# Filter taps and spectra taken out of PSUM one round earlier in the odd attentions, the last heads rotated in two parts, one weight tile loaded before the filter table

## The reference

```python
def odd_mixer(h, positions, w_in, w_out, ...):
    u = h @ w_in                                   # 256 x 3072
    # 4 differential heads: q, k normed and rotated, two softmaxes each
    o_c = diff_causal_attention(qc, kc, vc, lam)   # p0 - lam * p1, times v
    o_c = rms_norm(o_c, diff_subln) * (1.0 - lam_init)
    # 8 block-attention heads; with 256 tokens there is one block: plain causal softmax
    qm = apply_rope(rms_norm(m[:, :, 0], moba_qn), positions)
    km = apply_rope(rms_norm(m[:, :, 1], moba_kn), positions)
    o_d = moba_attention(qm, km, m[:, :, 2])
    return concat([o_c, o_d]) @ w_out

def hyena_filters(L, w1, b1, w2, b2, w3, freq):    # second block, weights only
    h = sin(freq[1] * (sin(freq[0] * (feats @ w1 + b1)) @ w2 + b2))
    h = (h @ w3).reshape(L, 2, 2, 512)             # the "taps"
    h = h * exp(-t * deltas)                       # the window
    k = concat([h[:, :, 0], 0, h[:0:-1, :, 1]])
    return k / (sum(abs(k)) + EPS)
# long_conv later multiplies by rfft(k): the "spectra"

mod = silu(c) @ ada_w[layer] + ada_b[layer]        # modulation rows of each layer
```

## Time and profile before

| | us |
|---|---|
| median of 3 runs | 2554.66 |
| lowest and highest | 2551.91, 2556.96 |
| the profiled execution's own time | 2556.27 |
| its span in the profile | 2555.0 |
| TensorE busy | 2423.8 (95%) |
| VectorE busy | 1792.0 (70%) |
| ScalarE busy | 1227.1 (48%) |
| GpSimd busy | 392.2 (15%) |

### The profile page before, as it was taken

One profiled execution on the slowest core, in us unless ns is written; L12 is line 12 of the kernel. 1 busy time (PEld: TensorE's weight loads), 2 busy tenths in 40 slices (PEclk: granted clock), 3 DMA queues, 4 the chain that ended last, 5 costly groups with the idle time before them and its releaser, 6 DMA issues.

```text
span 2555.0 us, 27667 instructions
## 1 busy us (share of the span) xinstructions
PE 2423.8 (95%) x11093; PEld 1796.7 (70%) x11093; DVE 1792.0 (70%) x2019; ACT 1227.1 (48%) x1453; POOL 392.2 (15%) x434
## 2 busy tenths in 40 slices
PE   6987999998899999999999989999999999999998
PEld 2455797644469877454798658787878787878786
DVE  4576577585459766355665348888888888888887
ACT  1142453222135431122443247676767676767675
POOL 1045371131027210044221000000000000000000
PEclk9978999996899999999999999999999999999999
DMA  7631468642056777203466339989898989898995
GB/s 302 268 148 50 165 264 306 232 162 97 33 206 231 302 284 294 91 1 132 174 256 230 128 115 343 368 322 368 317 368 321 369 321 368 322 366 321 368 347 216
DMA packets 50672, 631.01 MB, mean 247 GB/s; under 512 B 8696, under 2 KB 9385, under 8 KB 12713
## 3 DMA queue, kind: packets, MB, share of 16 engines
q1 hardware_dynamic: 44192, 619.47, 64.3%
q10 hardware_dynamic: 3960, 6.97, 0.8%
q0 software_dynamic: 2384, 2.73, 0.3%
HBM read 625.47 MB, written 3.67 MB: 246 GB/s over the span
## 4 chain that ended last, share of the span: by engine, by line
PE 81%; DVE 9%; ACT 3%; issue 3%; DMA 3%; POOL 1%; ACTq 0%; SPq 0%; DVEq 0%; POOLq 0%
PE psum L1137 18%; PE psum L1138 18%; PE psum L1139 18%; PE psum L1032 4%; PE psum L1005 4%; PE psum L2460 3%; DVE sbuf L702 3%; PE psum L2454 2%; PE psum L1221 2%; PE psum L2039 1%; PE psum L1172 1%; DMA ring<-in_t_ada 1%; PE psum L2951 1%; PE psum L742 1%; DVE ring_r L1132 1%
## 5 line engine op out<-in xcount | busy, mean ns | idle before, releaser
L1138 PE MATMUL psum<-ring_r,sc_r 128*128 128x512 f32 x1688 | 665.8, 394 | 0.0
L1132 DVE TENSOR_TENSOR ring_r<-ring,sbuf_r 128x2048 fp32r<-128x2048 f32 (+1 forms) x287 | 538.4, 1880 | 174.4 <-ACT sbuf_r L1123 173.3
L1123 ACT CAST sbuf_r<-ring 128x2048 fp32r<-128x2048 f32 (+1 forms) x287 | 445.5, 1555 | 347.7 <-PE psum L1139 259.8
L1132 DVE TENSOR_TENSOR ring_r<-ring,sc_r 128x2048 fp32r<-128x2048 f32 (+1 forms) x243 | 478.3, 1974 | 137.9 <-ACT sc_r L1123 137.1
L1123 ACT CAST sc_r<-ring 128x2048 fp32r<-128x2048 f32 (+1 forms) x243 | 397.9, 1642 | 269.8 <-PE psum L1139 233.1
L1137 PE MATMUL psum<-sbuf_r,sc_r 128*128 128x512 f32 (+1 forms) x1148 | 428.7, 373 | 4.5 <-DVE sc L2784 3.4
L1138 PEld LDWEIGHTS psum<-ring_r,sc_r 128*128 128x128 f32 x1688 | 317.4, 188 | 72.9 <-issue 3.1
L702 DVE SCALAR_TENSOR_TENSOR sbuf<-ring,sbuf 128x512 f32<-128x512 f32 x404 | 327.2, 817 | 28.3 <-DMA ring<-in_t_ada 22.9
L1139 PE MATMUL psum<-sbuf_r,sc_r 128*128 128x512 f32 x860 | 340.2, 396 | 0.0
L1137 PE MATMUL psum<-sc_r 128*128 128x512 f32 x828 | 333.4, 403 | 0.7 <-DVE sc_r L2983 0.7
L1139 PE MATMUL psum<-sc_r 128*128 128x512 f32 x828 | 324.2, 392 | 0.0
(11 more groups left out here) (333 smaller groups left out, 2890.1 us busy)
## 6 DMA issues: line engine op xcount, KB each, us to landing
ring<-in_t_moe SPq DMA_DIRECT2D x168, 2048.0 KB, 8.0
ring<-in_t_ada SPq DMA_DIRECT2D x48, 2048.0 KB, 10.0
ring<-in_t_mlp SPq DMA_DIRECT2D x32, 2048.0 KB, 8.2
ring<-in_t_win SPq DMA_DIRECT2D x17, 2048.0 KB, 10.0
ring<-in_t_ffn SPq DMA_DIRECT2D x16, 2048.0 KB, 8.3
ring<-in_t_out SPq DMA_DIRECT2D x7, 2048.0 KB, 8.3
ring<-in_t_bias SPq DMA_DIRECT2D x2, 2048.0 KB, 9.9
spectra<-sc POOLq DMA_DIRECT2D x5, 512.0 KB, 2.9
```

What stands on the lines that cost most here:

```text
L1123: p.act.e.copy(p.r(hi), src).then_inc(*p.sig("high", st.tag, n))
L1132: p.dve.e.tensor_tensor(p.r(src), src, p.r(hi), ALU.subtract).then_inc(*p.sig("lowp", st.tag, n))
L1138: e.matmul(out, l[0], r[1], start=False, stop=False)
```

## The change

Six edits. VectorE takes taps and spectra out of PSUM at the end of the round in which TensorE makes them, no longer after the maximum of the next round; the products now stand ahead of them in the round. `act_absolute` comes one round earlier, and so the sum stands in round 12 and the second spectrum in round 13. The norms come in rounds 13 and 14. The heads h3 are rotated in two parts: sums, scale and the first two of five steps in round 5, the other three in round 6. No products stand in rounds 4, 5, 6, 13 and 14 (before: none in 5 and 15). In the list of loads ada 25 stands ahead of fk.

```diff
@@ -405,7 +405,7 @@
                   ("out0", 1)]
         loads += self.among_mlp("mlp0", 13)
         loads += self.among("win1", range(6), 1, range(22, 25))
-        loads += [("fk", 0), ("ada", 25), ("out2", 0), ("ada", 26), ("out2", 1)]
+        loads += [("ada", 25), ("fk", 0), ("out2", 0), ("ada", 26), ("out2", 1)]
         loads += self.among_mlp("mlp1", 27)
         loads += self.among("win2", range(6), 1, range(36, 42))
         loads += [("fu", 0), ("gm", 0), ("bias", 0), ("bias", 1), ("out4", 0), ("out4", 1)]
@@ -1616,7 +1616,7 @@
     ins.then_inc(*p.sig("rope", name))
 
 
-def rotate(p, E, side, tag, src, rs, name, b, dr, t1, t2):
+def rotate(p, E, side, tag, src, rs, name, b, dr, t1, t2, parts=(0, 1)):
 
     e = E.e
     ta, tb, _, _ = p.rope[name]
@@ -1624,9 +1624,12 @@
     q1 = v3(t1[:, 0:n * d], n)
     q2 = v3(t2[:, 0:n * dr], n)
     h = dr // 2
-    E.wait_ge(*p.at("rope", name))
-    E.link(e.tensor_tensor(src, src, bc(rs, 2, [128, n, d]), ALU.mult))
-    e.tensor_tensor(q1, src, bc(ta[:, b, :], 1, [128, n, d]), ALU.mult)
+    if 0 in parts:
+        E.wait_ge(*p.at("rope", name))
+        E.link(e.tensor_tensor(src, src, bc(rs, 2, [128, n, d]), ALU.mult))
+        e.tensor_tensor(q1, src, bc(ta[:, b, :], 1, [128, n, d]), ALU.mult)
+    if 1 not in parts:
+        return
     e.tensor_tensor(q2[:, :, 0:h], src[:, :, d - h:d], bc(tb[:, b, 0:h], 1, [128, n, h]), ALU.mult)
     E.link(e.tensor_tensor(q2[:, :, h:dr], src[:, :, d - dr:d - h], bc(tb[:, b, h:dr], 1, [128, n, h]), ALU.mult))
     if d > dr:
@@ -1991,9 +1994,11 @@
 
 
 
-SPECTRUM = {8: ("tap", (0, 1, 2)), 9: ("tap", (3, 4, 5)), 10: ("tap", (6, 7)), 11: ("fk", (0,)), 12: ("fk", (1,)),
-            13: ("sum", (0, 1)), 14: ("fk", (2,)), 15: ("fk", (3, 4)), 16: ("fk", (5, 6)), 17: ("fk", (7,)),
+SPECTRUM = {8: ("tap", (0, 1, 2)), 9: ("tap", (3, 4, 5)), 10: ("tap", (6, 7)), 11: ("fk", (0,)), 12: ("sum", (0, 1)),
+            13: ("fk", (1,)), 14: ("fk", (2,)), 15: ("fk", (3, 4)), 16: ("fk", (5, 6)), 17: ("fk", (7,)),
             18: ("fk", (8, 9))}
+
+SPECTRA = {14: (0, 1), 15: (2, 3, 4), 16: (5, 6), 17: (7,), 18: (8, 9)}
 
 
 def fk_bank(p, u):
@@ -2147,7 +2152,7 @@
         if r == 9:
             p.pe.wait_ge(*turn_at(p, "h2", 1))
             pe_sums(p, 25)
-        if r == 13:
+        if r == 12:
             p.pe.wait_ge(*p.at(*moved(p, p.accs[24][1])))
         pe_spectrum(p, r)
         if r in (15, 16):
@@ -2174,17 +2179,18 @@
     return 16 * i, 16 * i + 16
 
 
-def dve_heads(p, i):
+def dve_heads(p, i, parts=(0, 1)):
     base, name = p.BASES[i]
     c0, c1 = odd_stats(i)
-    for b in range(2):
-        p.dve.wait_ge(*p.at("hsq", i, b))
-        p.dve.e.tensor_reduce(p.SQ[:, c0 + 8 * b:c0 + 8 * b + 8], v3(p.SQT2[b], 8), X_AXIS, ALU.add).then_inc(
-            *p.sig("hss", i, b))
-    p.dve.wait_ge(*p.at("hss", i, 1))
-    dve_rstd(p, f"h{i}", p.SQ[:, c0:c1], p.RQ[:, c0:c1], 64)
+    if 0 in parts:
+        for b in range(2):
+            p.dve.wait_ge(*p.at("hsq", i, b))
+            p.dve.e.tensor_reduce(p.SQ[:, c0 + 8 * b:c0 + 8 * b + 8], v3(p.SQT2[b], 8), X_AXIS, ALU.add).then_inc(
+                *p.sig("hss", i, b))
+        p.dve.wait_ge(*p.at("hss", i, 1))
+        dve_rstd(p, f"h{i}", p.SQ[:, c0:c1], p.RQ[:, c0:c1], 64)
     rotate(p, p.dve, "D", f"h{i}", v3(p.U[:, 0, base:base + 512], 8), p.RQ[:, c0:c0 + 8], name, 0, 64,
-           p.TMP2[0], p.TMP2[1])
+           p.TMP2[0], p.TMP2[1], parts)
 
 
 def act_heads(p, i):
@@ -2260,20 +2266,8 @@
             dve_put(p, "u1", u, U[:, 0, 256 * u:256 * u + 512], 512)
         if r == 4:
             dve_turn(p, "h2", p.AT[2], 4, [7])
-        if r == 5:
-            dve_heads(p, 3)
-        what, which = SPECTRUM.get(r - 1, ("", ()))
-        if what == "tap":
-            for u in which:
-                dve_window(p, u)
-        if r in (14, 15):
-            dve_norms(p, r - 14)
-        if r == 15:
-            for u in range(3):
-                dve_spectrum(p, u)
-        elif r > 15 and what == "fk":
-            for u in which:
-                dve_spectrum(p, u)
+        if r in (5, 6):
+            dve_heads(p, 3, (r - 5,))
         if r == 10:
             dve_columns(p, 25)
         if r == 12:
@@ -2285,8 +2279,16 @@
             dve_rstd(p, "o", p.SQ[:, 64:72], p.RQ[:, 64:72], 128)
         if r == 17:
             dve_turn(p, "ot", p.HT, 4, [7], p.SUBF)
-        if r != 5:
-            dve_products(p, 2 if r != 15 else 0, 27)
+        if r not in (4, 5, 6, 13, 14):
+            dve_products(p, 2, 27)
+        what, which = SPECTRUM.get(r, ("", ()))
+        if what == "tap":
+            for u in which:
+                dve_window(p, u)
+        if r in (13, 14):
+            dve_norms(p, r - 13)
+        for u in SPECTRA.get(r, ()):
+            dve_spectrum(p, u)
     dve_columns(p, 26)
     dve_turn(p, "mt", p.HT[:, 4:8, :], 4, [7])
     dve_products(p, 40, 27)
@@ -2359,14 +2361,14 @@
             act_put(p, "u1", u, U[:, 1, 256 * (u - 1):256 * (u - 1) + 512], 512)
         if r == 4:
             act_heads(p, 3)
+        if r == 10:
+            act_absolute(p, 0)
         if r == 11:
             p.act.wait_ge(*p.at("uout", 7))
             for b in range(2):
                 e.activation(v3(p.SQT2[b], 4), v3(p.XN[:, b, 0:512], 4), ACT.Square).then_inc(*p.sig("osq", b))
-            act_absolute(p, 0)
+            act_absolute(p, 1)
             act_root(p, "o", p.SQ[:, 64:72])
-        if r == 12:
-            act_absolute(p, 1)
         if r == 16:
             act_turn(p, "ot", p.HT, 4, [7], p.SUBF)
         if r == 18:
```

## The result

| | before | after |
|---|---|---|
| median of 4 runs each, us | 2555.81 | 2529.97 |
| lowest and highest | 2551.91, 2557.13 | 2527.76, 2534.68 |
| profiled execution, own time | 2556.27 | 2527.76 |
| its span | 2555.0 | 2526.4 |
| ratio of the times, 95% interval | | 0.9906, [0.9889, 0.9922] |

The change makes the kernel faster by 0.94% (0.78 to 1.11), about 24 us; 2532.8 was predicted. TensorE is busy 2410.9 us in the page of after, 12.9 less: the work is the same, so these are matmuls that now run at the higher clock. The rest is waits. One of the executions behind the tables of this document, of products_in_4, ran in a slow state (2732.5 us); it counts in that kernel's median and not in its ratio.

A forecast was written before the change was run, and what follows sets the result against it. The prediction took TensorE, busy 95% of the span, to bound the kernel. Gains of 6.5 + 4.2 + 11.2 = 21.9 us from a median of 2554.66 gave 2532.8 us, range 2526 to 2541.

The forecast's parts named there:

- Rounds 4 to 6: Up to h3's transposes: TensorE's waits fall from 5.6 to 1.6 us and the clock stays up; 6.5 us gained.
- the step with a choice in it: Rounds 4 to 6: 3.9 us gained if the clock falls all the same, 8.1 if no wait is left.
- The swap: Loading ada 25 ahead of fk is worth nothing beside the edits that take products out of round 4.
- The split rotation: Rounds 6 and 7: rotating h3 in two parts costs 0, at most 0.9 + 1.6 = 2.5 us.
- Taps: Rounds 8 to 11: waits of 1.8 and 2.4 go, round 8's 1.9 stays, clock unchanged; 4.2 us gained.
- The rival of taps at 2.4 GHz: Tap rounds run at full clock, half of 25 us more gained, about 2521 us; chance 0.04.
- Sum, norms and spectra: Rounds 11 to 16: waits of 1.78 and 5.82 and the slow clock go; 11.2 us gained.
- the tightest place: First spectrum's way out, for which round 15's spectrum waits: VectorE has 0.7 us to spare.
- Behind the rounds: After the rounds, eight products are left instead of two; cost 0, at most 0.5 us.
- The clock didn't fall elsewhere: Rival: waits go but TensorE's slow stretches come at other places; 15.7 us gained, 2539.0; chance 0.11.
- the bound: Rival: VectorE becomes the bound in rounds 8 to 18, 30 us lost against 21.9 gained, 2562.8; chance 0.03.
- round 7 has no wait: Rival: rotation and mixing late by 2.5 us, new wait in round 7, clock falls; 16.8 gained, 2537.9; chance 0.06.

The follow-up runs named there:

- products_in_4: The changed kernel with the two products of round 4 put back; median 2534.55 us, ratio to before 0.9927.
- early_half: The kernel before with only the swap of loads, the split rotation and no products in rounds 4 to 6; 2547.42 us, ratio to before 0.9978.
- sums_later: copy_root with the one-column sums (L742) moved from round 9 to behind round 11's spectrum; 2513.39 us, ratio to before 0.9844.
- copy_root: The changed kernel with ScalarE's last-projection copy ahead of round 8's exponentials and h3's root behind round 5's exponentials and copy; 2518.48 us.
- filler: copy_root with one unread matmul of 128 rows and 512 columns ahead of the taps of rounds 8, 9 and 10; 2524.36 us.
- heads_whole: The changed kernel with h3 rotated whole in round 5 again; 2530.45 us, ratio to before 0.9906.

## Why the prediction was right

**Rounds 4 to 6, 6.5 us.** It measured 6.4. A wait of 1.8 is left where 1.6 was forecast, it is the only one in these rounds, and both projections take 3.65, so the clock stayed up. That was the step with a choice in it (3.9 to 8.1), and early_half confirms it by itself with 6.6.

**The swap, nothing.** Right as it was put, beside the other edits. Alone it isn't nothing (3.5 us of the rounds), because it frees VectorE's wait of 5.89 by 2.5.

**The split rotation, 0 to 2.5.** The mechanism was right and the sizes were a little off. The three steps took 1.5 us and not 2; the mixing took 1.1 more, inside the 1.59 allowed for it. GpSimd's last step took 1.26, not 1.59, since VectorE was less in its way. TensorE came to h3 at 587.52 and waited for nothing. The rule that the prediction took from the Trainium skill ("SBUF — State Buffer", "Who interferes with whom"), that the later one stands until the first is done, fits the trace in its stronger form: L1444 and the mixing ended 0.02 and 0.28 us behind GpSimd's steps. Which of the two came first the trace doesn't settle; the mixing's record begins 0.03 us ahead of GpSimd's (583.08, 583.11).

**Taps, 4.2 us.** Measured 3.9. The waits of 1.8 and 2.4 are gone, the 1.9 of round 8 is there to the tenth, and the clock was at 0.50 as before, from 597 to 627 against 607 to 641. The 0.3 us less are mostly its earlier fall in round 8's taps (3.97 for 3.33). The prediction called it unknown and said that waits alone don't explain it. The experiments name two things that start the low stretch, the wait in round 8 and the one-column sums, neither of which the change touches. That it stayed low was thus taken over from the kernel before and not derived. The rival of taps at 2.4 GHz describes a state that this code can have: sums_later has it, with the wait gone and the sums moved.

**Sum, norms and spectra, 11.2 us.** Measured 11.5. VectorE's timeline of after for the tightest place, from the maximum of round 14 to the first spectrum's way out:

```profile
646.27 0.42 DVE L1426 TENSOR_REDUCE sbuf<-psum 128x2 f32<-128x256 f32 x1 [0.32 <-PE psum L1387]
...
647.91 3.35 DVE L2065 RECIPROCAL sc<-sc 128x512 f32<-128x512 f32 x1
651.30 1.29 DVE L2073 TENSOR_TENSOR sc<-psum,sc 128x512 f32<-128x512 f32 x2
```

The first of the two merged spectra was out at about 651.95 (half of 1.29 behind 651.30), and TensorE began round 15's spectra at 652.34. So 0.4 us were to spare and not 0.7; the forecast had little room for error here.

**Behind the rounds, 0 to 0.5.** Right: eight products and the remainder, then the first residual multiplies, and the one after them waits for TensorE anyway:

```profile
698.86 5.75 DVE L702 SCALAR_TENSOR_TENSOR sbuf<-ring,sbuf 128x512 f32<-128x512 f32 x8
...
708.49 0.69 DVE L1052 TENSOR_TENSOR sc<-psum,sbuf 128x512 f32<-128x512 f32 x1 [1.54 <-PE psum L1032]
```

**The rivals.** The clock didn't fall elsewhere behind the rounds' waits (1.00 from 628 to 680), VectorE is named at none of the places that would have shown it as the bound (L1402 names it once, with 0.8 us in round 2, before as after), and round 7 has no wait. The sum of the terms was 21.9 for 21.7 measured. The median came out 2.8 us below the forecast, which no step explains but the 1.1 of the output projection and the spread of the code that wasn't touched.

## What to carry to other kernels

Read what stands ahead of a short wait on the engine that is waited for: here nearly every one of TensorE's waits was for a small copy or a way out of PSUM that was queued behind something nobody needed yet, and several cost their own length and then more at half clock. Where the granted clock is low although TensorE is busy, look at the small matmuls and the wait in front of the stretch, not only at its own instructions. Here moving the small ones behind a large group helped, and filling in more work did not. And judge an edit of 5 us by the stretch between two instructions that it can affect; the time of the unchanged kernel before moved by 8 us between its runs (2549.44 to 2557.26).

## What the runs showed of the chip

- Eight one-column matmuls (16 records) ahead of 64-row matmuls went with a drop of the granted clock to 0.53 and 0.50 over 18 us in which TensorE was busy 18.00 us (copy_root, filler). Moved behind a 128-row spectrum, the taps ran at 1.00 and the drop was short (0.83 over 10 us).
- A wait of 1.93 us in front of the same taps was followed by 30 us at half clock (after); a wait of 1.80 ahead of a large projection (round 6) by none; one of 2.90 ahead of the same projection was followed by a drop (5.35 us for 3.65, products_in_4).
- A VectorE operation with two inputs in SBUF took 1.57 us for 0.49 when a GpSimd step of 1.26 us began beside it, one of a single column 0.78 for 0.22 beside a step of 0.72, and GpSimd's own steps took 0.73, 0.72 and 1.26 us in after and 0.90, 0.90 and 1.60 where VectorE did its own steps of the rotation beside them (heads_whole).
- A change from the root to the exponentials on ScalarE cost one table load of 1.28 us (after, 578.10; the exponential starts at 579.39, 1.30 behind the root's end).
